# The chunked recurrence of a transformer block: the inverse on four quadrants of the tensor array, the state 64 columns wide

## The reference, cut to what matters

```
def step(state, inp):                       # state: 64 x 64 per head
    r_t, w_t, k_t, v_t, a_t, b_t = inp
    sa = einsum('bhvk,bhk->bhv', state, a_t)
    state = state * w_t + sa[..., None] * b_t + v_t[..., None] * k_t
    return state, einsum('bhvk,bhk->bhv', state, r_t)
...
_, y = lax.scan(step, zeros(...), xs, reverse=reverse)      # 512 steps
```

## Time and profile before

| | us |
|---|---|
| median of 3 runs | 3643.03 |
| lowest and highest run | 3634.65, 3651.44 |
| the profiled execution | 3634.89 |
| its span, first to last instruction | 3632.9 |

### The profile page before, as it was taken

The page is one execution under the profiler, slowest core; times in us unless marked ns, Lnnn a source line. Parts: engine busy times, 40 slices in busy tenths (PEclk is TensorE's granted clock), DMA queues, the critical chain, the costliest instruction groups (busy, mean ns, idle before and its releaser), DMA issues.

```text
span 3632.9 us, 42105 instructions
## 1 busy us (share of the span) xinstructions
PE 2871.9 (79%) x16406; PEld 1464.6 (40%) x16406; DVE 1599.7 (44%) x3317; ACT 994.5 (27%) x2377; POOL 701.5 (19%) x618
## 2 busy tenths in 40 slices
PE   7689978888699999999998987777787555655555
PEld 6467766625633333333334773433343111111111
DVE  3643653446400110011002336655566766777674
ACT  2222222232100000000001415565444334433342
POOL 0411412000000000000000003323334444444442
PEclk9898999778799999999999898997788777778777
DMA  2210220212499999999995358987899999999997
GB/s 108 71 68 19 77 82 8 99 64 117 198 380 420 419 420 420 420 419 420 420 420 234 113 192 350 406 324 280 340 372 402 420 419 420 420 419 419 420 419 327
DMA packets 155991, 1068.75 MB, mean 294 GB/s; under 512 B 17296, under 2 KB 19088, under 8 KB 30352
## 3 DMA queue, kind: packets, MB, share of 16 engines
q0 software_dynamic: 75408, 543.20, 36.8%
q1 hardware_dynamic: 80384, 522.87, 35.6%
HBM read 1052.63 MB, written 13.37 MB: 293 GB/s over the span
## 4 chain that ended last, share of the span: by engine, by line
PE 57%; DMA 23%; DVE 12%; ACT 6%; issue 2%; POOL 0%; SPq 0%; DVEq 0%; ACTq 0%; POOLq 0%
PE ps L92 54%; DMA gb<-in_peer_uv,eidx 21%; DVE gb L146 3%; PE ps L97 2%; DMA ring<-in_wt 1%; ACT dots L168 1%; ACT L168 1%; ACT diag L168 1%; DVE inv_tt L115 1%; DVE wa_hi L130 1%; DVE wa_lo L115 1%; DVE expert_act L115 1%; DVE rw_t L134 1%; POOL gb L86 0%; DVE x L115 0%
## 5 line engine op out<-in xcount | busy, mean ns | idle before, releaser
L92 PE MATMUL ps<-gb,diag 64*64 64x512 f32 x4096 | 692.2, 795 | 486.5 <-ACT diag L168 480.5
L146 DVE CUSTOM_DVE_ANT_0 gb<-gb,xn 128x1024 f32<-128x1024 f32 x512 | 625.7, 1223 | 326.9 <-DMA gb<-in_peer_uv,eidx 295.8
L86 POOL DMA_INDIRECT gb<-in_peer_uv,eidx x512 | 554.0, 1082 | 1076.2 <-PE ps L92 819.6
L92 PEld LDWEIGHTS ps<-gb,diag 64*64 64x64 f32 x4096 | 147.5, 161 | 952.3 <-ACT diag L168 867.8
L92 PE MATMUL ps<-ga,xt 128*64 128x512 f32 x1120 | 330.9, 601 | 2.5 <-DVE xt L120 2.5
L115 DVE TENSOR_TENSOR expert_act<-expert_act,ps 128x512 f32<-128x512 f32 x32 | 22.0, 687 | 540.5 <-PE ps L92 539.9
L168 ACT ACTIVATE dots<-dots 128x1 f32<-128x1 f32 (+1 forms) x346 | 70.3, 203 | 663.3 <-DVE dots L146 647.1
L115 DVE TENSOR_TENSOR x<-x,ps 128x512 f32<-128x512 f32 (+1 forms) x96 | 61.4, 643 | 415.2 <-PE ps L92 414.6
L168 ACT ACTIVATE diag<-cons,dots 128x128 f32<-128x128 f32 x512 | 205.5, 401 | 39.3 <-ACT dots L168 1.1
L92 PEld LDWEIGHTS ps<-ga,xt 128*64 128x64 f32 x1120 | 118.7, 137 | 187.3 <-issue 180.1
L92 PE MATMUL ps<-h_hi,wa_hi 128*128 128x512 f32 x368 | 161.0, 437 | 41.3 <-DVE wa_lo L115 38.1
(11 more groups left out here) (315 smaller groups left out, 3826.3 us busy)
## 6 DMA issues: line engine op xcount, KB each, us to landing
ring<-in_wt SPq DMA_DIRECT2D x77, 1024.0 KB
ga<-in_eg SPq DMA_DIRECT2D x70, 1024.0 KB, 26.3
ga<-in_eu SPq DMA_DIRECT2D x70, 1024.0 KB, 27.0
ga<-in_ed SPq DMA_DIRECT2D x68, 1024.0 KB, 27.7
gr<-in_eu SPq DMA_DIRECT2D x37, 1024.0 KB, 27.3
gr<-in_ed SPq DMA_DIRECT2D x34, 1024.0 KB, 27.7
ring<-in_eg SPq DMA_DIRECT2D x29, 1024.0 KB, 26.7
gr<-in_eg SPq DMA_DIRECT2D x29, 1024.0 KB, 27.3
```

Of the source, the lines that this page charges most:

```text
L86: self.e.indirect_dma_start(out, None, table, bass.IndirectOffsetOnAxis(ap=idx, axis=0)).then_inc(s, 16)
L92: i = self.e.matmul(out, l, r, start=st, stop=sp, skip_group_check=True)
L146: self.done(self.e.tensor_tensor_reduce(out=o, in0=a, in1=b, scale=scale, scalar=start, op0=o0, op1=o1, accum_out=acc), name)
```

## The change

All of it is in the recurrence.

1. **The crossed half.** TT and X1 of chunk q now lie on the other half of the partitions, `HALF[1 - q]`, while Tm and B stay. The update of TT (X1 and TT, output on their own half) and the update of TB (TT and X1, output crossed) then use different quadrants for the same q and head. They are issued in turn, two quadrants each, with one signal for both.
2. **The first inverse** is written by VectorE to X1; twelve products (six with the identity as weights, six with it as moving operand) make its transpose in TB[g] and its crossed copy in a bank of the turn, and VectorE copies the latter to TT.
3. **`tok` of AR** is six products with 64 output columns each that put the two halves crosswise, in place of three transposes. mv is crossed, dec and u0 read the crossed half.
4. **The state** is 64 columns wide. u is six products 64x64 into two banks; s is twelve products 64x64; y is eighteen products 64x64, with the state's part in one bank and the rest in another.
5. **VectorE** now takes u in two instructions, the state in two instructions half as wide, whose second multiplies by `decay_end` read with a broadcast; POOL makes no decay mask. y is evicted by VectorE in both directions, in two instructions (a copy and an add for d = 0, two adds for d = 1). ScalarE no longer evicts y.
6. **Turns**: u and y take two banks instead of one, and the first inverse one bank for each g.

The core of the diff:

```diff
 def pe_matrix, the first inverse:
-            pe.wait_ge(("tt", d, j, 0, g))
+            b, use, before = turn.next()
+            pe.wait_ge(("z", d, j, g), *before)
...
-                for q in HALF:
-                    pe.mm(PS[TB[g]][q, 64 * n:64 * n + 64], TT[q, 3 * g + n, :], ident[q, q], n == 0, False,
...
+                for q in range(2):
+                    z = X1[HALF[q], 3 * g + n, :]
+                    pe.mm(PS[TB[g]][HALF[q], nc_], z, ident[HALF[q], HALF[q]], n == 0, False)
+                    pe.mm(PS[b][HALF[1 - q], nc_], ident[HALF[q], HALF[q]], z,
+                          name=("t_ps", d, j, 0, g) if (n, q) == (2, 1) else None)
 the two updates of a level:
-                quads(PS[b], g, X1, TT, ("dt_ps", d, j, n, g))
-                if n < 5:
-                    quads(PS[TB[g]], g, TT, X1, ("t_ps", d, j, n, g), False)
+                for i in range(3):
+                    for q in range(2):
+                        x, tt = X1[HALF[1 - q], 3 * g + i, :], TT[HALF[1 - q], 3 * g + i, :]
+                        last = (i, q) == (2, 1)
+                        if n < 5:
+                            pe.mm(PS[TB[g]][HALF[q], 64 * i:64 * i + 64], tt, x, False, True)
+                        pe.mm(PS[b][HALF[1 - q], 64 * i:64 * i + 64], x, tt, name=("t_ps", d, j, n, g) if last else None)
 def pe_chunks, u:
-                pe.mm(PS[b][r, 128 * p:128 * p + 128], At[:, p, r], S0[:, p, :], name=("u_ps", d, n) if p == 2 else None)
+                for e in range(2):
+                    pe.mm(PS[banks[e]][r, 64 * p:64 * p + 64], At[HALF[e], p, r], S0[HALF[e], p, :],
 s:
-                pe.mm(PS[b][:, pc], ATok[r, 1, pc], U[r, pc], True, False)
-                pe.mm(PS[b][:, pc], ATok[r, 2, pc], ATok[r, 3, pc], False, True, name=("s_ps", d, n) if p == 2 else None)
+                for e in range(2):
+                    hc = slice(64 * (2 * p + e), 64 * (2 * p + e) + 64)
+                    pe.mm(PS[b][HALF[e], pc], ATok[r, 1, hc], U[r, hc], True, False)
+                for e in range(2):
+                    hc = slice(64 * (2 * p + e), 64 * (2 * p + e) + 64)
+                    pe.mm(PS[b][HALF[e], pc], ATok[r, 2, hc], ATok[r, 3, hc], False, True,
 y:
-                pe.mm(PS[b][:, oc], S0[:, p, :], AR[:, p, j, 128 + 64 * q:192 + 64 * q], True, False)
...
+                    pe.mm(PS[banks[0]][HALF[e], oc], S0[HALF[e], p, :], AR[HALF[e], p, j, 128 + 64 * q:192 + 64 * q])
+                    pe.mm(PS[banks[1]][HALF[e], oc], U[r, 64 * h:64 * h + 64], M4[r, h, 64:128], True, False)
 def dv_chunks:
-            dv.wait_ge(("decay", d, n))
-            dv.tt(S1, S1, PCM, MUL, name=use)
+            dv.tt(S1, S1, PC[:, :, n:n + 1].to_broadcast([128, 3, 64]), MUL, name=use)
...
+            if d == 0:
+                o = yS[:, :, 64 * n:64 * n + 64]
+                dv.cp(o, heads(PS[b0][:, 0:192]), name=use0)
...
+            dv.tt(o, heads(PS[b1][:, 0:192]), o, ADD, name=use1)
```

More of the change, by code:

```diff
@@ L718, in ac_matrix @@
         for g in range(2):
+            turn.next()
             t_out(0, g)
@@ L772, in dv_matrix @@
         for g, q in enumerate(HG):
-            level(dv, TT, q, 0, M4)
-            dv.tt(TT[:, q, :], TT[:, q, :], row3(eye, 3), ADD, name=("tt", d, j, 0, g))
+            b, use, _ = turn.next()
+            dv.wait_ge(("t_ps", d, j, 0, g))
+            dv.cp(TT[:, q, :], heads(PS[b][:, 0:192]), name=use)
+            dv.mark(("tt", d, j, 0, g))
             yield
@@ L810, in pe_chunks @@
             n = 2 * j + q
-            r = slice(64 * q, 64 * q + 64)
+            r = HALF[q]
             S0 = SS[n % 2]
-            b, use, before = turn.next()
-            pe.wait_ge(("at", d, j, q), ("state", d, n - 1) if n else ("zero_state", d), *before)
+            banks = []
+            for e in range(2):
+                b, use, before = turn.next()
+                pe.wait_ge(("at", d, j, q), ("state", d, n - 1) if n else ("zero_state", d), *before)
+                banks.append(b)
             for p in range(3):
-                pe.mm(PS[b][r, 128 * p:128 * p + 128], At[:, p, r], S0[:, p, :], name=("u_ps", d, n) if p == 2 else None)
+                for e in range(2):
+                    pe.mm(PS[banks[e]][r, 64 * p:64 * p + 64], At[HALF[e], p, r], S0[HALF[e], p, :],
+                          name=("u_ps", d, n) if (p, e) == (2, 1) else None)
             yield
@@ L839, in dv_chunks, with every2 @@
         U0 = bufs(j)[3]
+        def every2(ap, e):
+            return ap.rearrange("p (a e b) -> p a e b", e=2, b=64)[:, :, e, :]
         for q in range(2):
             n = 2 * j + q
-            r = slice(64 * q, 64 * q + 64)
+            r = HALF[q]
             S0, S1 = SS[n % 2], SS[1 - n % 2]
-            b, use, _ = turn.next()
             dv.wait_ge(("u_ps", d, n), ("u0", d, j))
-            dv.tt(U[r, :], PS[b][r, 0:384], U0[r, :], ADD, name=use)
+            for e in range(2):
+                b, use, _ = turn.next()
+                dv.tt(every2(U[r, :], e), heads(PS[b][r, 0:192]), every2(U0[r, :], e), ADD, name=use)
             dv.mark(("u", d, n))
@@ L865, in ac_chunks @@
         for q in range(2):
-            n = 2 * j + q
-            turn.next()
+            turn.next(), turn.next()
             yield
@@ L870, in ac_chunks @@
             yield
-            b, use, _ = turn.next()
-            if d == 0:
-                ac.wait_ge(("y_ps", d, n))
-                ac.act(yS[:, :, 64 * n:64 * n + 64], PS[b][:, 0:192].rearrange("p (a b) -> p a b", a=3), ACT.Copy, name=use)
-                ac.mark(("y", d, n))
+            turn.next(), turn.next()
             yield
     def po_chunks(po, d, j):
-        for q in range(2):
-            n = 2 * j + q
-            po.wait_ge(("prep", d))
-            if n:
-                po.wait_ge(("state", d, n - 1))
-            po.tt(PCM, row3(cons[:, C_BD:C_BD + 128], 3), PC[:, :, n:n + 1].to_broadcast([128, 3, 128]), MUL, name=("decay", d, n))
-            for _ in range(3):
-                yield
+        for _ in range(6):
+            yield
     mx = A("mem_x", 0, 2, 1024)
```

80 lines of the change are left out of this document (44 added, 36 removed).

## The result

| | median us | lowest to highest | ratio to before, 95% interval |
|---|---|---|---|
| before | 3643.91 (4 runs) | 3634.65 to 3651.44 | |
| changed | 3588.48 (4 runs) | 3579.33 to 3589.76 | 0.9844, 0.9816 to 0.9872 |

The change saves 55 us, 1.6%, with an interval of 1.3 to 1.8%; 51 were forecast, and 3592. The profiled execution of the changed kernel took 3589.8 us, its span 3587.6.

A forecast was written before the change was run, and what follows sets the result against it. TensorE's products were taken to bound the recurrence, the cut passing on in full. Gains of 19.8 + 14.6 + 18.7 + 3.4 = 56.5 us, less losses, became 51: 3592 us against the median 3643.0, range 3572 to 3620.

The forecast's parts named there:

- The updates, 19.8: Inverse levels 1 to 4: 64 pairs of updates fall from 0.70 to 0.39 us on four quadrants, saving 19.8 us.
- s, y and u, 36.7: Chunk steps: 64x64 products on quadrants save 14.6 us in s, 18.7 in y and 3.4 in u.
- Given back, 5.5: Losses of 2.1, 1.2 and 1.0 us (copy waits, last block, first inverse and tail), plus something for two-bank turns.
- read out long before: Two-bank turns: u and y wait for one more bank, claimed to be already read out; only something allowed for it.
- up to 5 us: Shortened products lying in half-clock stretches of the two stages give double, up to 5 us more.
- The wait as long as now: Sign in the changed profile: TensorE's wait for the first inverse stays as long as before, on `inv_x`.
- the likeliest case: The forecast itself: a gain of 38 to 65 us, chance 63%; with the same waits, mean clock stays at 0.9.
- fifth rival: Shorter products leave TensorE waiting more, half clock stays on through the blocks: slower, 3692 us with 100 more; chance 4%.
- The first: Rival: the two updates do not run together, as both row halves share each bank; gain 31, 3612 us; chance 9%.
- The second: Rival: products of s and y on the same rows do not pair; 14 us less gain, 3606 us; chance 5%.
- The third: Rival: waits in level transitions (6 us) and for filler casts (14 us) replace the products; gain 31, 3612; chance 10%.
- The fourth: Rival: four quadrants keep the array denser, half of the 58.8 us at half clock goes; 15 more, 3577; chance 9%.

The follow-up runs named there:

- updates_only: The changed kernel with the chunk steps (u, s, y, wide state, POOL's decay mask) of the kernel before, so the crossed inverse alone; 3626.3 us, ratio 0.9964.
- state_masks: The kernel before with the changed chunk steps, and POOL's masked B waiting for both first inverses of a block; 3574.5 us, ratio 0.9818.
- masks_fill2: The changed kernel with POOL's masks behind the first inverse and two filler units instead of one behind step 2 of each block; 3577.9 us, ratio 0.9816.

## Why the prediction was right, point by point

- **What bounds the stage.** TensorE's products did: a cut of 56.5 in their prices, 51 with what was to be given back, shortened the stages by 57.3 in one profile and the program by 55.4 at the medians. Nothing behind the recurrence took it back.
- **The updates, 19.8.** The step of 0.39 came as forecast. The whole term, less its waits, was to be about 17; with POOL's masks moved and the clock's share taken out it is 14 to 16, so it was taken some 2 us too high.
- **s, y and u, 36.7.** 36.3 at the medians without and 37.9 with the moved masks, about 34 in the stages with the clock's share taken out.
- **Given back, 5.5.** Its parts did not come as listed. ScalarE's copies made TensorE wait for 1.1 us in all (`inv_t` 0.8, `inv_x` 0.3), where 2.1 were put down between levels 3 and 4 alone. The second bank of u and y, "read out long before", may be what cost 1.09 twice. The sum has the first inverse's twelve products eight times; they stand there sixteen times, 0.3 us more. Against this stands the overlap at the seams, which the sum lacked: X, y and updates took 2.07 for 2.24.
- **Why 55 to 57 and not 51.** Mostly the clock: 10 us less at half clock is about 5 us, and 57.3 less 5 is 52. The prediction named this, "up to 5 us" where the shortened products lie at half clock, and left it out of its sum. That the rest fits within 1 us is luck, with the updates 2 us too high and the seams left out.
- **The first inverse.** "The wait as long as now" held, 25.6 for 23.2. The prediction saw that its instructions take 1.10 us beside POOL's work, and took that as given. The row of 0.66 for the same size, and 0.36 for the same number of elements, should have made it ask what the wait costs and whether POOL can be moved. It answered only that POOL's decay mask did not stand there; the five masks did.
- **The clock.** The mean stayed at 0.91, as the likeliest case had it. The prediction's fifth rival was not seen in the changed kernel; in `updates_only` a part of it was, 39 us more at half clock.
- **Rivals.** The first fell with the 0.39; the Trainium skill's sentence that row tiles cannot access one PSUM bank at the same time (TensorEngine Tiling (Array Packing), Restrictions and Gotchas) does not hold here for tiles that write different halves of its partitions: both banks of the updates get both row halves, four products at a time. The second fell with s: in `state_masks` its first product starts at 263.90 and the first update behind it at 264.60, 0.70 for twelve products on one half of the rows. The price of the second rival was too low: if y's products run one after the other on their half of the rows, the six of the state's part among them, y costs about 0.6 more, as s does, and not 0.27; the gain lost would be 20 us and not 14. The third did not come. The fourth did not come by its own mechanism, a denser array: half clock went when the wait for the inverse was cut, in the kernel before (60 to 24) as in the changed one (50 to 13). The rows of s, for the second rival:

```profile
263.90 0.27 PE L92 MATMUL ps<-u_a,tok 64*64 64x64 f32 x1
...
264.60 0.27 PE L92 MATMUL ps<-inv_tt,inv_x 64*64 64x64 f32 x1
```

## What to carry to other kernels

In this kernel small products paid by the quadrant they needed, so put the halves of operands such that groups that follow each other in the list lie on different quadrants; the order inside a group mattered little. Before costing an instruction at its measured length, compare it with others of the same size in the same trace: one that takes three times as long may have a neighbour on another engine that holds it, and a wait that moves that neighbour was worth half a redesign here. An idle stretch of TensorE costs more than its length when half clock follows it, so a part whose worth is in question is measured best in a version where that stretch is small, and with the time at half clock beside it.

## What the runs showed of the hardware that was not expected

- A product on free quadrants starts before some that stand ahead of it in the list and need other quadrants: 0.18 us behind the first of six, which take 0.35.
- VectorE's `tensor_tensor` of 128x192 float32 from SBUF takes 0.36 us alone and 1.10 beside POOL's `tensor_tensor` of 128x384; `u_a`, with one operand from PSUM (64x192), takes 0.36 beside it too. POOL's take about 1.0 in either kernel. All the loss is on VectorE's side.
- Half clock followed the wait for the inverse, but not in proportion: 50 us of it in the two stages with 25.6 us of such waits, 10 with 11.6, and 13 with 6.5, but 99 with 22.7 in `updates_only` and 34 with 10.2 in `masks_fill2`. Which waits bring it on, and what ends it, was not settled.
